# Logits of the odd attention: one product of whole fp32 operands, or three passes over split ones

## The reference, cut to what matters

```python
def odd_layer(hn, ...):                       # 1024 tokens, 8 query heads of 128, 2 key heads
    q, k, v, gate, qi, ki, wi = split_cols(hn @ w_in, ODD_SPLITS)
    q = rms_norm(q.reshape(bsz, L, 8, 128), q_g)
    k = rms_norm(k.reshape(bsz, L, 2, 128), k_g)
    att = dsa_attention(q, k, v, qi, ki, wi, rel_bias)   # softmax(q k^T / sqrt(128) + bias, on the chosen keys) v
    return (att * jax.nn.silu(gate)) @ w_out
```

## Time and profile before

| | us |
|---|---|
| median of three runs | 2040.41 |
| the profiled execution | 2038.71 |
| its span in the profile | 2037.5 |
| TensorE busy | 1969.8 (97%) |
| VectorE busy | 1431.8 (70%) |
| ScalarE busy | 885.3 (43%) |
| GpSimd busy | 656.3 (32%) |
| all logits passes of VectorE (L2291), 64 | 48.3 |
| all sums of bias and mask of GpSimd (L2496), 48 | 72.2 |

### The profile page before, as it was taken

The page is one execution under the profiler, slowest core; times in us unless marked ns, Lnnn a source line. Parts: engine busy times, 40 slices in busy tenths (PEclk is TensorE's granted clock), DMA queues, the critical chain, the costliest instruction groups (busy, mean ns, idle before and its releaser), DMA issues.

```text
span 2037.5 us, 24547 instructions
## 1 busy us (share of the span) xinstructions
PE 1969.8 (97%) x9256; PEld 1515.3 (74%) x9256; DVE 1431.8 (70%) x2169; ACT 885.3 (43%) x1589; POOL 656.3 (32%) x476
## 2 busy tenths in 40 slices
PE   7999999999999999999999999999999999999997
PEld 6778766787648776666688777888787877778885
DVE  7667768513179997355427699899998887685539
ACT  5343366333356861344312333443326765362431
POOL 3677610452201211445444000000002673235443
PEclk9999999999999999999999999999999999999999
DMA  6322340342411122211053201121123213465322
GB/s 268 121 63 77 93 158 22 124 176 89 126 45 32 42 83 76 100 52 42 11 196 105 91 33 62 43 72 52 53 103 124 80 71 136 142 213 207 104 92 104
DMA packets 72431, 197.94 MB, mean 97 GB/s; under 512 B 11182, under 2 KB 20559, under 8 KB 71800
## 3 DMA queue, kind: packets, MB, share of 16 engines
q1 hardware_dynamic: 72168, 196.35, 28.1%
q10 hardware_dynamic: 144, 0.00, 0.0%
HBM read 152.89 MB, written 46.71 MB: 98 GB/s over the span
## 4 chain that ended last, share of the span: by engine, by line
PE 61%; DVE 19%; ACT 3%; issue 2%; POOL 1%; DMA 0%; DVEq 0%; ACTq 0%; SPq 0%
PE psum L266 58%; DVE m L2950 7%; PE psum L269 3%; DVE m L321 1%; DVE m L2971 1%; DVE m L2172 1%; DVE m L531 1%; DVE m L540 1%; DVE m L3149 1%; ACT m L301 1%; ACT m L395 1%; DVE m L3088 1%; DVE m L456 1%; DVE m L3152 1%; POOL m L311 0%
## 5 line engine op out<-in xcount | busy, mean ns | idle before, releaser
L266 PE MATMUL psum<-m,m 128*128 128x512 f32 (+9 forms) x8456 | 1886.9, 392 | 35.2 <-DVE m L321 9.5
L266 PEld LDWEIGHTS psum<-m,m 128*128 128x128 f32 (+3 forms) x8456 | 1429.0, 186 | 464.2 <-issue 145.1
L311 POOL TENSOR_TENSOR m<-m,m 128x1024 fp32r<-128x1024 f32 (+1 forms) x122 | 307.0, 2521 | 981.8 <-ACT m L301 981.5
L301 ACT ACTIVATE m<-m 128x1024 fp32r<-128x1024 f32 (+2 forms) x166 | 173.6, 1048 | 339.5 <-PE psum L266 214.9
L2950 DVE SCALAR_TENSOR_TENSOR m<-m,m,m 128x1024 f32<-128x1024 f32 x240 | 312.5, 1304 | 6.3
L269 PE MATMUL psum<-m,m 128*128 128x128 f32 x784 | 110.2, 276 | 19.3 <-ACT m L1446 6.0
L269 PEld LDWEIGHTS psum<-m,m 128*128 128x128 f32 x784 | 89.8, 141 | 39.9 <-ACT m L1446 8.0
L2172 DVE TENSOR_SCALAR_CACHE_REDUCE m<-m,m 128x896 bf16<-128x896 f32 (+4 forms) x130 | 102.8, 848 | 1.1
L2291 DVE CUSTOM_DVE_ANT_0 m<-psum,m 128x128 f32<-128x128 f32 (+3 forms) x64 | 48.3, 755 | 45.3 <-PE psum L266 22.8
L2386 ACT ACTIVATE m<-m,m 128x1024 bf16<-128x1024 f32 (+1 forms) x62 | 64.1, 1036 | 23.3 <-DVE m L2199 23.3
L2496 POOL TENSOR_TENSOR m<-m,m 128x384 f32<-128x384 f32 (+5 forms) x48 | 72.2, 1524 | 3.7 <-DVE m L2291 3.7
(11 more groups left out here) (308 smaller groups left out, 1663.0 us busy)
## 6 DMA issues: line engine op xcount, KB each, us to landing
m<-in_w SPq DMA_DIRECT2D x164, 512.0 KB, 3.4
scr_hscr<-m SPq DMA_DIRECT2D x4, 2048.0 KB, 6.6
m<-scr_hscr SPq DMA_DIRECT2D x4, 2048.0 KB, 10.5
scr_turned<-scr_strip SPq DMA_DIRECT2D x8, 575.5 KB, 12.3
m<-in_x SPq DMA_DIRECT2D x4, 1024.0 KB, 8.2
scr_gscr<-m SPq DMA_DIRECT2D x16, 256.0 KB, 4.3
m<-in_x SPq DMA_DIRECT2D x2, 2048.0 KB, 8.8
m<-scr_turned SPq DMA_DIRECT2D x8, 512.0 KB, 3.5
```

The source lines that it names most:

```text
L266: return self.nc.tensor.matmul(out, lhsT, rhs, start=start, stop=stop, skip_group_check=True)
L301: k.nc.scalar.activation(k.hi[SLOT[i]][:, 0:kk * n], k.raw[i % 2][:, 0:kk * n], ACT.Copy).then_inc(*k.up("w_hi", i))
L311: k.nc.gpsimd.tensor_tensor(lo, raw, hi.bitcast(F32), ALU.subtract).then_inc(*k.up("w_lo", i))
```

## The change

Queries and keys of the odd attention are split. ScalarE writes the high part of query head n to `QH[n]` (`high_query`) and of key head kv to `KH[kv]` (`high_key`); VectorE writes the low part over the whole one (`low_query`, `low_key`). The logits are then `mm3` of the parts. A chunk is made at least 256 keys wide. Query head 0 and key 0 are split during the gates' projections; query n + 1 in the middle of head n, key 1 in the middle of head 2. Some tiles move: the second bias strip and the third probability tile, and with the strip its load on SP, which now waits for the last gate's store and comes behind gate 0's load.

```diff
-        self.strips = [k.tile(H0 + o * KB, [1024]) for o in (20, 8)]
-        self.pr = [k.tile(H0 + o * KB, [1024]) for o in (24, 28, 12)]
+        self.strips = [k.tile(H0 + o * KB, [1024]) for o in (20, 16)]
+        self.pr = [k.tile(H0 + o * KB, [1024]) for o in (24, 28, 8)]
+        self.QH = [k.tile(H0 + 12 * KB, [1024], F32R)] + [k.tile(X0 + (32 + 4 * n) * KB, [1024], F32R) for n in range(1, 8)]
+        self.KH = [k.tile(O + 4 * KB * i, [1024], F32R) for i in range(2)]
+        self.QL, self.KL = self.MH, k.tile(PH + 32 * KB, [2, 1024], F32R)
 # tensor_odd, s1
-        pe.wait_ge(*at("head", n, b // 4))
-        for half in range(b // 4 + 1):
-            pe.wait_ge(*at("head", 8 + n // 4, half))
+        kv, bs = n // 4, slice(128 * b, 128 * b + 128)
+        pe.wait_ge(*at("q_lo", n))
+        pe.wait_ge(*at("k_lo", kv))
         for c, e in O.chunks(b):
-            ins = k.mm(k.bank(bank + c // 512)[:, 0:e - c], O.QT[:, n, 128 * b:128 * b + 128], O.KT[:, n // 4, c:e], True, True)
+            e = max(e, c + 256)
+            ins = k.mm3(k.bank(bank + c // 512)[:, 0:e - c], (O.QH[n][:, bs], O.QL[:, n, bs]),
+                        (O.KH[kv][:, c:e], O.KL[:, kv, c:e]), True, True)
 # vector_odd
+    def low_query(n):
+        dve.wait_ge(*at("q_hi", n))
+        V.tensor_tensor(O.QL[:, n], O.QT[:, n], O.QH[n].bitcast(F32), ALU.subtract).then_inc(*up("q_lo", n))
+    def low_key(kv):
+        dve.wait_ge(*at("k_hi", kv))
+        V.tensor_tensor(O.KL[:, kv], O.KT[:, kv], O.KH[kv].bitcast(F32), ALU.subtract).then_inc(*up("k_lo", kv))
 # in the loop over u, the projections
+        if u == 27:
+            low_key(0)
+    low_query(0)
 # s1
-        if (n, b) == (0, 2):
-            dve.wait_ge(*at("og_out", 6))
 # in the loop over i, behind s1 and s3, ahead of s2
+        if i % 8 == 5 and i < 56:
+            low_query(i // 8 + 1)
+        if i == 21:
+            low_key(1)
 # scalar_odd
+    def high_query(n):
+        for half in range(2):
+            act.wait_ge(*at("head", n, half))
+        act.wait_ge(*at("og_ps", 7, 1)) if n else act.wait_ge(*at("og_out", 6))
+        act_parts(k, O.QT[:, n], O.QH[n], "q_hi", n)
+    def high_key(kv):
+        ...
+        act_parts(k, O.KT[:, kv], O.KH[kv], "k_hi", kv)
 # behind the gates' Silu
+            if (m, half) == (5, 1):
+                high_key(0)
+            if (m, half) == (7, 0):
+                high_query(0)
 # in the loop over i, behind s1 and s3, ahead of s2
+        if i % 8 == 4 and i < 56:
+            high_query(i // 8 + 1)
+        if i == 20:
+            high_key(1)
 # sync_odd
-            sp.wait_ge(*at("head_norm", O.norms[-1]))
+            sp.wait_ge(*at("og_out", 7))
-    load_strip(1)
     sp.wait_ge(*at("og_ps", 7, 1))
     load_gate(0)
+    load_strip(1)
     sp_panel(k, PANEL_AT["og7"] + 6)
```

More of the change, by code:

```diff
@@ L2430, in scalar_odd @@
         act_panel(k, PANEL_AT[f"oq{m}"] + 4)
+    def high_query(n):
+        for half in range(2):
+            act.wait_ge(*at("head", n, half))
+        if n:
+            act.wait_ge(*at("og_ps", 7, 1))
+        else:
+            act.wait_ge(*at("og_out", 6))
+        act_parts(k, O.QT[:, n], O.QH[n], "q_hi", n)
+    def high_key(kv):
+        for half in range(2):
+            act.wait_ge(*at("head", 8 + kv, half))
+        if kv:
+            act.wait_ge(*at("keep", 5))
+        else:
+            act.wait_ge(*at("head_ss", 7))
+        act_parts(k, O.KT[:, kv], O.KH[kv], "k_hi", kv)
     for m in range(8):
```

## The result

The changed kernel takes 2047.13 us (median of five runs, 2046.65 to 2050.21); the kernel before took 2038.44 beside it (five runs, 2038.04 to 2041.76). The ratio is 1.0041 [1.0027, 1.0056]: slower, by 8.4 us (0.4%). The forecast was 2043.6 with a range of 2036 to 2050, and +3.2 us over the median then shown. The mechanism that it named is there; two terms were missed.

A forecast was written before the change was run, and what follows sets the result against it. TensorE, 97% busy, was taken to bound the kernel, except stretch A, set by GpSimd's chain. Head 0 -0.85, five heads +3.50, head 2 +3.74, head 7 -0.36, D -2.66: +3.4 us, forecast 2043.6, range 2036 to 2050.

The forecast's parts named there:

- A: Head stretch with logits of blocks 4 to 6, 5.57 us: set by GpSimd's chain, so 0.62 us less TensorE work gains 0.
- Price of three passes: Logits matmuls: three passes cost 0.353, 0.517 and 0.680 us at 256, 384 and 512 columns.
- D: Head stretch with logits of blocks 1 to 3 and value products, 9.95 us: 0.38 less in seven heads, -2.66.
- Rival 4: Logits blocks: format changes cost up to 0.34 us a block where TensorE sets the pace, up to +7; 7%.
- The meeting on SBUF: Mid-head: VectorE's 1.22 us subtraction waits for GpSimd's block 6 sum, ends at 979.65 and delays the copy to 980.26.
- B: Head stretch with block 7's logits, reciprocals and value products of blocks 0 to 3: from 5.04 to 5.74 us, +0.70.
- Rivals 2 and 3: Subtraction mid-head: rival 2, no meeting on SBUF, 2037.6 us, 13%; rival 3, VectorE starves, 2056.5 us, 11%.
- 2.9 us or so: Sign to look for: length of the new VectorE subtraction mid-head, in place of 1.22 us.
- Start: Query 0 and key 0 split under the gates' projections: first logits could start about 832.9, cost 0.
- Head 2: Key 1's subtraction queues behind the query's: +3.04 more there, +3.74 in the sum, +3.36 with D's share.
- Heads 1 and 3 to 6: Repeating heads: +0.70 each in B, forecast +0.32 each overall, about 22.87 us a head.
- Outside the attention: Rest of the kernel beyond the odd attention: forecast change 0.

The follow-up runs named there:

- e1: The changed kernel with the splits of a head's next query and of key 1 moved two blocks earlier; ratio 0.9985 to the kernel before.
- e5: The changed kernel with high parts in place of low ones and a one-column memset for each subtraction; ratio 0.9979 to the kernel before.
- e7: e1 with GpSimd's sum of block 5 put ahead of its low part of the output; 2032.72 us, ratio 0.9958 to the kernel before.
- e2: The changed kernel with each subtraction replaced in place by a VectorE instruction reading one SBUF tensor; ratio 0.9987 to the kernel before.
- e4: The changed kernel with whole fp32 products back for the logits, splits left in place (maximum for subtraction); ratio 1.0050 to the kernel before.
- e8: The kernel before with only GpSimd's order changed, block 5's sum ahead of the low part of the output; ratio 0.9979 to the kernel before.

## Why the prediction was right, and which terms were mis-sized

- **What bounds a head.** Right. A is held by GpSimd's chain, not by TensorE: TensorE's work in it fell by 0.49 (0.62 worked out) and A stayed (5.59), as in e1 and e5. When that chain's order is changed (e7), A falls to 4.86.
- **Price of three passes.** Right: 0.36 for 256 columns and 0.53 for 384 in the chain of the changed kernel (0.353 and 0.517 worked out), D 9.61 against 9.57. Rival 4 is out.
- **The meeting on SBUF.** Right in kind and size: the sum had the subtraction from 977.76 to 979.65, 1.89 us, and it took 1.92; with one input 1.21 (e2). B came to 5.76 against 5.74; had the blocked instruction paid its whole time after the wait, the sum would have had 5.90. Rivals 2 and 3 are out. "2.9 us or so" in my list of signs was a slip against that sum. TensorE's idle times came out at 0.67 and 0.78 (0.8 and 1.1 said). The second is a matter of the records: from start to start it is 939.38 - 936.95 = 2.43, less 1.36 for six matmuls of 0.2267, and 1.07 is what I meant.
- **Start.** Right: the first pass over logits starts at 833.12, where it started at 833.16.
- **Head 2.** The mis-sized term inside the attention. Of +5.03 my sum had +3.36. The queue of two subtractions was right (3.13 us for the second; e4's head 2 is +3.08 over the others, the sum +3.04). Missing was what a wait of 3.8 us does to TensorE's clock: 1.6 us on the sixteen products behind it.
- **Heads 1 and 3 to 6** gave 0.08 more than forecast, five times; in head 3, 0.02 each in A and B, 0.04 in D.
- **Outside the attention** I had put 0; it is about +3. The traces put most of it down to TensorE's clock. Stretches at half clock (1.2 GHz) come at different places from run to run. Every trace has one at its very end. Leaving that one out, they fill 4.6 us of the part behind the attention on average in the three traces of before, and 10.2 us in the three of the changed kernel. Where TensorE sets the pace, an us at half clock loses half an us of work, so by that estimate the 5.7 us more cost 2.8 of the 2.9 us. Over all fourteen traces, too, this part is on the whole longer the more time it spends at half clock. It is not the whole: e4 has 3.4 us at half clock there, like the first trace of before, and 1037.3 us against 1034.2. The turns that VectorE and GpSimd take around 1810 to 1885 us differ as well, and were not tested. What lets the clock fall more often in the changed kernel, or whether three traces against three are chance, is not shown. By the ratio e4 and e7 show +3.1 and e2 and e8 none, which fits no single step of the change.
- **The verdict.** "Within 0.2%" was the likeliest with 0.52, slower had 0.37. With the two missing terms, 1.6 and about 3, the forecast of +3.4 becomes the measured 8, past the bound. That 2047.13 lies only 3.5 us from the forecast owes something to luck: the median shown was 2 us above the one measured beside the change (2040.41 against 2038.44), and the difference itself was missed by 5. There are two slips besides: 2040.41 + 3.4 is 2043.8 and not 2043.6, and the sums take 0.16 us off a blocked instruction where rows 6 gave 0.14. Neither matters.

Where did the gain go? The products alone are worth 0.65 us a head (e5). The subtraction in its place takes back 1.05: 0.36 by its length, 0.69 by its meeting with GpSimd. Two blocks earlier it takes nothing.

## What to carry to other kernels

Before a step is put into a pipeline, look at which engine's copy TensorE waits for next, and at what GpSimd reads from SBUF in that moment: the same 1.2 us subtraction cost 1.05 us a head in one place and nothing in another (even where it took 2.45 us), and an instruction as long with one input cost 0.36 in the first. Cheaper matmuls pay only in stretches where the chain of waits runs through them; here a swap of two GpSimd instructions, with cheaper products and a better place for the splits, was worth more than the products by themselves (11.7 us in the attention against 4.9). The swap alone gave 3.6 us there on the kernel before, and 7.9 on top of e1, where TensorE had less to do in that stretch. Two added steps in one queue should be spread before anything else: the wait that they make together can also cost the clock of what comes after.

## What the runs showed of the hardware that I had not expected

- A TensorE idle of 3.83 to 3.86 us was followed by products at half clock in three traces of three (4.77 to 5.01 us instead of 3.31); one of 3.44 us at the same place was not (3.32).
- A short wait costs more than itself. Without the 0.16 us idle ahead of block 7's logits, the stretch from it to the end of the twenty records is 0.42 us shorter (e8): with no wait the first record starts 0.16 us before the last transpose ends, and the twenty take 0.10 less. Between e1 and e7, too, the same 22 records end 0.26 us sooner, counted from the end of what stands ahead of them, than the idle time explains.
- VectorE and GpSimd, both with queued instructions on two SBUF inputs, take turns, and the one that waits gets the next: 1.92 for a subtraction of 1.22 us, 3.13 for the one queued behind it, and 2.71 (e1, head 0) or 2.45 (e7) where it comes just after a sum has begun.
